# Turned products in the 64-wide attention heads: values stand in TensorE, the divided maps stream

## The reference, cut to what matters

```
p   = softmax(scores)            # rows: 128 queries, columns: up to 256 keys
out = p @ v                      # v: keys x 64
y   = out @ w_proj_a             # or w_out
```

## Time and profile before

| what | value |
|---|---|
| median of 3 runs | 1392.94 us (1392.09 to 1394.0) |
| profiled execution | 1392.42 us, span 1390.6 us |
| mean granted clock | 0.998 |
| PE busy | 99% of the span |
| DVE busy | 68% of the span |
| ACT busy | 51% of the span |

### The profile page before, as it was taken

How to read it: one execution, slowest core, us unless ns; L and a number is a source line. 1 busy time by engine, 2 the same in 40 slices (tenths; PEclk the granted TensorE clock), 3 DMA queues, 4 the chain that set the end, 5 groups by cost and what they waited for, 6 DMA issues and landing times.

```text
span 1390.6 us, 19203 instructions
## 1 busy us (share of the span) xinstructions
PE 1374.7 (99%) x7399; PEld 1170.1 (84%) x7399; DVE 943.3 (68%) x1161; ACT 712.6 (51%) x920; POOL 129.2 (9%) x141
## 2 busy tenths in 40 slices
PE   8999999999999999999999999999999999999999
PEld 7988888888888888888888888888888877788887
DVE  6895667666677666766567666766667778766665
ACT  5556436444455444576654444544445666554442
POOL 4100002000030000032020000200000321300000
PEclk9999999999999999999999999999999999999999
DMA  8644457655555556543255555466555532455562
GB/s 281 176 153 152 152 182 264 220 184 200 189 174 190 181 183 198 188 156 122 92 181 188 198 187 183 165 200 198 192 184 179 170 133 91 150 198 197 181 194 78
DMA packets 164859, 246.34 MB, mean 177 GB/s; under 512 B 4952, under 2 KB 121860, under 8 KB 164672
## 3 DMA queue, kind: packets, MB, share of 16 engines
q1 hardware_dynamic: 162256, 240.14, 51.5%
q0 software_dynamic: 1776, 4.74, 1.2%
q10 hardware_dynamic: 768, 0.66, 0.2%
HBM read 244.45 MB, written 1.07 MB: 177 GB/s over the span
## 4 chain that ended last, share of the span: by engine, by line
PE 91%; DVE 4%; ACT 2%; issue 1%; POOL 1%; DMA 0%; SPq 0%; ACTq 0%; POOLq 0%
PE ps L1542 27%; PE ps L1509 15%; PE ps L1547 14%; PE ps L1511 14%; PE ps L1510 14%; PE ps L1777 2%; PE ps L1748 1%; DVE wlo L901 1%; PE ps L1535 1%; ACT whi L552 1%; DVE xx L946 1%; ACT pr L617 1%; PE ps L2025 0%; DMA raw<-in_w_in 0%; ACT xx L589 0%
## 5 line engine op out<-in xcount | busy, mean ns | idle before, releaser
L1542 PE MATMUL ps<-xx,whi 128*128 128x512 f32 x1760 | 422.7, 391 | 1.6 <-DVE wlo L901 1.6
L1542 PEld LDWEIGHTS ps<-xx,whi 128*128 128x128 f32 x1760 | 325.4, 188 | 67.1 <-DVE wlo L901 2.6
L906 DVE TENSOR_TENSOR wlo<-raw,whi 128x2048 fp32r<-128x2048 f32 x120 | 275.1, 2293 | 94.2 <-ACT whi L560 94.2
L560 ACT ACTIVATE whi<-raw 128x2048 fp32r<-128x2048 f32 x120 | 229.6, 1913 | 122.4 <-PE ps L1511 122.4
L552 ACT ACTIVATE whi<-raw 128x2048 fp32r<-128x2048 f32 (+1 forms) x135 | 204.7, 1530 | 86.2 <-PE ps L1511 82.5
L1547 PEld LDWEIGHTS ps<-xx,wlo 128*128 128x128 f32 x1760 | 227.6, 191 | 9.9
L1547 PE MATMUL ps<-xx,wlo 128*128 128x256 f32 x1760 | 230.6, 283 | 0.0
L1509 PE MATMUL ps<-whi,hhi 128*128 128x512 f32 x504 | 198.6, 394 | 0.0
L1510 PE MATMUL ps<-wlo,hhi 128*128 128x512 f32 x504 | 196.7, 390 | 0.0
L1511 PE MATMUL ps<-whi,hlo 128*128 128x512 f32 x504 | 196.3, 390 | 0.0
L901 DVE TENSOR_TENSOR wlo<-raw,whi 128x2048 fp32r<-128x2048 f32 x75 | 171.4, 2287 | 24.8 <-ACT whi L552 24.7
(11 more groups left out here) (259 smaller groups left out, 1394.2 us busy)
## 6 DMA issues: line engine op xcount, KB each, us to landing
raw<-in_ffn_w_gate SPq DMA_DIRECT2D x44, 1024.0 KB, 5.2
raw<-in_ffn_w_up SPq DMA_DIRECT2D x44, 1024.0 KB, 5.1
raw<-in_ffn_w_down SPq DMA_DIRECT2D x44, 1024.0 KB, 4.8
raw<-in_w_in SPq DMA_DIRECT2D x40, 1024.0 KB, 5.1
raw<-in_w_gate_up SPq DMA_DIRECT2D x22, 1024.0 KB, 5.0
raw<-in_w_out SPq DMA_DIRECT2D x12, 1024.0 KB, 4.8
raw<-in_w_down SPq DMA_DIRECT2D x11, 1024.0 KB, 4.8
raw<-in_w_mem_kv SPq DMA_DIRECT2D x4, 1024.0 KB, 5.1
```

The source lines that it names most:

```text
L560: act.activation(whi[:, c % 3, :], raw[:, c % 3, :], ACT.Copy).then_inc(hi_done, 1)
L906: dve.tensor_tensor(wlo[:, c % 3, :], raw[:, c % 3, :], whi[:, c % 3, :], ALU.subtract)\
L1542: return pe.matmul(ps[:, bank + n, :], whi[:, slot, 256 * k + P * n:256 * k + P * n + P], both, start=start, stop=False)
```

## The change

- The list of A items runs over head pairs first and row tiles second, so that the first four items fill one bank.
- Items of kinds A and R, and X in layer 0 (24 items, `DIRECT`), are divided before they are turned: DVE's new `normalise(i)` makes the reciprocal of the two sums and multiplies the map in place. `item_turn` waits for it (`pn_ready`) and no longer for the exponential.
- In `item_pv` these items have v (128 keys x 64) standing and `pT` (128 queries) streaming. The heads e = 0 and 1 write the partitions 0 to 63 and 64 to 127 of one bank. The product comes out turned.
- The turns of `xn` in the first model (parts 0 and 1) and all four in layer 0 go, with the divisions in L1256 and L1440 for these items. ACT and DVE split straight from the product's bank (bank 7; bank 1 in layer 0). In the first model this is done in the iterations k = 5 and 9, where the divisions stood.
- In layer 0 the slots of turns and products move: `T_AT` is S + 3 for the first eight items, `V_AT` is S + 4 apart from items 8 to 11. Layer 1 stays as it was.

```diff
-ITEMS = [("A", rt, a, -1) for rt in range(RT) for a in range(AH // 2)]
+ITEMS = [("A", rt, a, -1) for a in range(AH // 2) for rt in range(RT)]
+DIRECT = [k in "AR" or (k == "X" and layer == 0) for k, _, _, layer in ITEMS]
+NORMED = np.cumsum(DIRECT).tolist()
-T_AT, V_AT = tuple(h + 2 for h in S_AT), tuple(h + 3 for h in S_AT)
+T_AT = (tuple(h + (3 if i < 8 else 2) for i, h in enumerate(S_AT)), tuple(h + 2 for h in S_AT))
+V_AT = (tuple(h + (3 if 8 <= i < 12 else 4) for i, h in enumerate(S_AT)), tuple(h + 3 for h in S_AT))
-Y_TURNS = ({40: 0, 43: 1, 53: 2, 57: 3}, {40: 0, 43: 1, 54: 2, 57: 3})
+Y_TURNS = {40: 0, 43: 1, 54: 2, 57: 3}
+Y_OUT = {V_AT[0][4 * g + 3] + 1: g for g in range(4)}
...
 # ScalarE, first model, after exps(k)
+                    if k in (5, 9):
+                        b = (k - 5) // 4
+                        act.wait_ge(pv_ready, 4 * b + 4)
+                        act.activation(hhi[:, b, :], ps[:, 7, :], ACT.Copy).then_inc(xhi_done, 2)
...
 # ScalarE, layer 0, at the head of a slot
+                    if L == 0 and h in Y_OUT:
+                        g = Y_OUT[h]
+                        act.wait_ge(pv_ready, i0 + 4 * g + 4)
+                        act.activation(y_hi_at[g], halves(ps[:, 1, :]), ACT.Copy).then_inc(y_hi, 1)
...
 # VectorE
+            def normalise(i):
+                kind, r, a, L = ITEMS[i]
+                nk = SEQ if kind == "X" else P * (r + 1)
+                total = sums[:, 2 * i:2 * i + 2]
+                v = halves(pr[:, i % 2, :])[:, :, 0:nk]
+                dve.wait_ge(p_ready, SOFT[i])
+                link(dve.reciprocal(total, total))
+                dve.tensor_tensor(v, v, total.unsqueeze(2).to_broadcast([P, 2, nk]), ALU.mult).then_inc(pn_ready, 1)
...
                 elif 7 <= u < 19:
+                    if 0 <= u - 8 < 8:
+                        normalise(u - 8)
                     scores(u - 7)
...
                     if k in (5, 9):
-                        link(dve.reciprocal(rec[:, 0:8], sums[:, 2 * i:2 * i + 8]))
-                        dve.wait_ge(pv_ready, i + 4)
-                        dve.tensor_tensor(xn[:, r, 0:512]..., ps[:, 7, :]..., rec[:, 0:8]..., ALU.mult)
+                        b = (k - 5) // 4
+                        dve.wait_ge(xhi_done, KC * T_Y0 + 2 * b + 2)
+                        dve.tensor_tensor(hlo[:, b, :], ps[:, 7, :], hhi[:, b, :], ALU.subtract).then_inc(xlo_done, 2)
...
                     if h in S_AT:
                         scores(i0 + S_AT.index(h))
+                    if L == 0 and h - 1 in S_AT:
+                        normalise(i0 + S_AT.index(h - 1))
...
 # TensorE, item_turn
+                elif DIRECT[i]:
+                    pe.wait_ge(pn_ready, NORMED[i])
                 else:
                     pe.wait_ge(p_ready, SOFT[i])
...
 # TensorE, item_pv
+                if DIRECT[i]:
+                    bank, col = 7 if L < 0 else 1, 256 * (a % 2) + P * r
+                    for b in range(nb):
+                        for e in range(2):
...
+                            c = P * (e * nb + b)
+                            ins = pe.matmul(ps[HD * e:HD * e + HD, bank, col:col + P], v, pT[:, i % 2, c:c + P],
+                                            start=(b == 0), stop=(b == nb - 1))
+                    ins.then_inc(pv_ready, 1)
+                    return
...
-                if u == 19:
-                    pe.wait_ge(sc_read, 12)
-                    pe.wait_ge(o_evac, 2)
-                    turn_part(T_Y0, 0, xn)
-                    turn_part(T_Y0, 1, xn)
...
-                    if h in Y_TURNS[L]:
-                        turn_product(Y_TURNS[L][h])
+                    if L == 1 and h in Y_TURNS:
+                        turn_product(Y_TURNS[h])
```

More of the change, by code:

```diff
@@ L585, in turned_gain @@
                     if c % 4 < 2:
-                        act.wait_ge(tr_ps, 4 * T + 2 * half + c % 2 + 1)
+                        act.wait_ge(tr_ps, turns_of(T) + 2 * half + c % 2 + 1)
                     else:
@@ L1283, in _ @@
                         lo(u + 3)
-                    if k == 12:
-                        for b in range(2):
-                            dve.wait_ge(xhi_done, KC * T_Y0 + 2 * b + 2)
-                            dve.tensor_tensor(hlo[:, b, :], ps[:, TURN_BANKS[T_Y0][b], :], hhi[:, b, :], ALU.subtract)\
-                                .then_inc(xlo_done, 2)
                     if 2 <= k < 6:
@@ L1410, in y_rest @@
                     dve.wait_ge(y_hi, 4 * L + g + 1)
-                    dve.scalar_tensor_tensor(out=y_lo_at[g], in0=halves(ps[:, Y_BANKS[g], :]),
+                    dve.scalar_tensor_tensor(out=y_lo_at[g], in0=halves(ps[:, Y_BANKS[g] if L else 1, :]),
                                              scalar=colg[:, 6:7] if L == 1 and g != 1 else 1.0, in1=y_hi_at[g],
@@ L1491, in _ @@
                         combine(i0 + S_AT.index(h))
-                    if h in V_AT and V_AT.index(h) % 4 == 3:
-                        group_out(V_AT.index(h) // 4)
+                    if L == 1 and h in V_AT[1] and V_AT[1].index(h) % 4 == 3:
+                        group_out(V_AT[1].index(h) // 4)
                 boundary(T_F2 + 3 * L, N_F2 + 3 * L, R_WO1 + 3 * L, WO[1 + L] + 3, None, FFU[2 + 2 * L])
@@ L1736, in item_turn @@
                     pe.wait_ge(pT_evac, i)
-                if L >= 0 and i - IT0[L] == 8:
+                if L == 1 and i - IT0[L] == 8:
                     pe.wait_ge(y_lo, 4 * L + 2)
@@ L1763, in item_pv @@
                     if g > 0 and (i - IT0[L]) % 4 == 0:
-                        pe.wait_ge(o_copied, 4 * L + g)
+                        if L == 0:
+                            pe.wait_ge(y_lo, g)
+                        else:
+                            pe.wait_ge(o_copied, g)
+                if DIRECT[i]:
+                    bank, col = 7 if L < 0 else 1, 256 * (a % 2) + P * r
+                    for b in range(nb):
+                        for e in range(2):
+                            h = 2 * a + e
+                            if kind == "X":
+                                v = kv[:, b, MW + HD * h:MW + HD * h + HD]
+                            elif L >= 0:
+                                v = z2[:, b, Z_V[g] + HD * h:Z_V[g] + HD * h + HD]
+                            else:
+                                v = z1[:, b, 2, HD * h:HD * h + HD]
+                            c = P * (e * nb + b)
[3 more added lines that the diff above has]
+                    return
                 for e in range(1 if kind == "D" else 2):
@@ L1774, in item_pv @@
                         else:
-                            v = z1[:, b, 2 if kind == "A" else 3, size * h:size * h + size]
+                            v = z1[:, b, 3, size * h:size * h + size]
                         c = P * (e * nb + b)
@@ L1927, in _ @@
                 pe.wait_ge(lo_done, u + 1)
+                if m == 0:
+                    pe.wait_ge(sc_read, 12)
                 if m == 1:
@@ L2017, in turn_heads @@
                         pe.wait_ge(heads_lo, 8 * L + k)
-                    if (g, which) == (3, "k"):
+                    if L == 1 and (g, which) == (3, "k"):
                         pe.wait_ge(y_lo, 4 * L + 1)
@@ L2053, in _ @@
                         item_scores(i0 + S_AT.index(h))
-                    if h in V_AT:
-                        item_pv(i0 + V_AT.index(h))
-                    if h in T_AT:
-                        item_turn(i0 + T_AT.index(h))
+                    if h in V_AT[L]:
+                        item_pv(i0 + V_AT[L].index(h))
+                    if h in T_AT[L]:
+                        item_turn(i0 + T_AT[L].index(h))
                     if h in HEAD_TURNS:
                         turn_heads(h)
-                    if h in Y_TURNS[L]:
-                        turn_product(Y_TURNS[L][h])
+                    if L == 1 and h in Y_TURNS:
+                        turn_product(Y_TURNS[h])
                 last_one(WO[1 + L] + 3, (4, 6), left(3), (y_lo, 4 * L + 4), T_F2 + 3 * L, R_WO1 + 3 * L)
```

50 lines of the change are left out of this document (22 added, 28 removed).

## The result

The changed kernel takes 1397.92 us (median of 6 runs, 1396.93 to 1399.73), the kernel before 1392.58 us in the same measurement (6 runs). The ratio is 1.0042, 95% interval 1.0032 to 1.0053: the medians lie 5.3 us apart, and the interval reaches from 4.5 to 7.4. I predicted 1398.5. Medians in this document are of executions in the usual state; two of the whole-array kernel in experiment 7 (1506 and 1941 us, mean granted clock 0.85 and 0.65) are left out.

A forecast was written before the change was run, and what follows sets the result against it. TensorE, busy 99% of the span, was taken as the bound. Products -0.8, turns -2.5, waits +7.7 and clock +1.7 gave +6.1 us on 1392.42: 1398.5 us, eight-in-ten range 1394 to 1407.5.

The forecast's parts named there:

- waits of items 0 to 5: First model: PE waits before turns for DVE's divisions, 2.8, 0, 0.8, 0.3, 0.5 and 3.3 us, +7.7 in all.
- turns: PE: eight transposes in the first model and sixteen in layer 0 go, -2.5 us.
- products: PE, 24 changed items: heads side by side, paying 0.2 or 0.3 us for the split array, -0.8 us.
- clock: PE's granted clock falls once behind the new long waits, +1.7 us (none 0, both +3.4).
- the circle over ACT and DVE: First model, items 1 to 4: scores, ACT's high part, DVE's low part, convolutions and division, then the turn; waits 0 to 0.8 us.
- The rival in which the normalising isn't late: First model: no waits on the division, only -0.8 and -2.5 us left, 1389.1 us; chance 0.11.
- the 0.31 of the scores: PE's scores, heads in two halves of the rows: going into the split array and out costs 0.31 us.
- One head after the other: Rival for the products on PE: pairs of records cost double, +8.4 us, 1406.9 us; chance 0.14.
- Bare pairs: Rival for the products on PE: the column split costs nothing, -6.8 instead of -0.8 us, 1392.5 us; chance 0.10.

The follow-up runs named there:

- experiment 7: The fifth version with both heads' values (128 columns) in the whole array, every sum started anew, half of each product thrown away: 1390.36 us (ten executions).
- experiment 8: The changed kernel with twelve transposes that nothing reads ahead of the turns of items 0 and 5: 1394.49 us, ratio 1.0016.
- experiment 4: The change in layer 0 alone, the first model as in the kernel before: 1388.43 us, ratio 0.9968.
- the fifth version: The changed kernel with the first model's divisions and bank 7 subtractions behind DVE's low part, and ScalarE's sine an iteration later: 1388.14 us, ratio 0.997.
- experiment 9: The changed kernel with only DVE's subtraction from bank 7 (k = 5 and 9) moved behind the low part: 1394.29 us, ratio 1.0013.
- experiment 3: The changed kernel with only item 0's division moved behind the low part: 1398.15 us, ratio 1.0039.
- experiment 1: The changed kernel with all the first model's divisions moved behind the low part of the same iteration, ahead of the convolutions: 1390.17 us, ratio 0.9977.
- experiment 11: The fifth version with the first model's products placed right behind the scores, ahead of the turns: 1386.09 us, ratio 0.9955.
- experiment 6: The fifth version with both heads' products in the same half of the array's columns, every sum started anew: 1395.58 us.
- experiment 2: The changed kernel with the first model's divisions and the subtraction from bank 7 both moved behind the low part: 1389.76 us, ratio 0.9975.

## Why the prediction was right

The sum, step by step. The measured values of work on PE come from distances inside one trace: item 0's turn to the end of the first model, and the stretch of layer 0.

| step | predicted | measured | from |
|---|---|---|---|
| waits of items 0 to 5 | +7.7 | +7.2 | waits of PE after |
| a wait of before that goes | not counted | -0.3 | item 1 waited 0.28 for its exponentials |
| turns | -2.5 | (-2.5) | not priced apart again |
| products | -0.8 | -2.5 | -5.0 in all, less the turns |
| clock | +1.7 | +3.4 | windows after; experiment 8 |
| sum | +6.1 | +5.3 | medians: +5.3 |

The traces close too. From the moment when PE is ready for item 0's turn to the first turn of layer 0 it is 534.51 us before (71.48 to 605.99) and 543.73 after (72.10 to 615.83), 9.2 more. Layer 0 is 4.0 less. That is +5.2, with the start of the kernel and layer 1 left out. That the median agrees to 0.1 is chance, since its interval is 2.9 us wide.

**The -5.0.** Layer 0 saves 4.03 (experiment 4). In the first model the fifth version takes 533.57 us with 0.32 of waiting, before 534.51 with 0.28: 0.98 saved. Together 5.0; less 2.5 for the turns, which were not priced apart again.

**The waits** were right item by item, within 0.2 us but for item 5, where 3.3 was predicted and 2.86 came. The causes were right too: item 0 waits for DVE's block of constants, items 2 to 5 for the circle over ACT and DVE, and item 5 also for ScalarE's copy (experiment 9). That they are one queue and not five separate waits is what experiment 3 adds: moving the first division alone doesn't pay, moving all of them does (experiment 1). What stands at the end of the queue can be taken out alone: item 5's wait got 1.8 us shorter and no other one longer (experiment 9). The rival in which the normalising isn't late predicted 1389.1; the kernel that makes it true comes to 1388.14.

**The products** were mis-sized: -0.8 in the sum, -2.5 measured. The heads run side by side with a cost for going in and out, as taken; the size of that cost is the term that was off. In the first model I took 0.3 and find 0.26, and had +0.3 us in all where 0.98 less 0.82 for the eight turns leaves -0.2. In layer 0 I took 0.2 for twelve items and 0.3 for four, 3.6 us together. It is 0.14 on the average of the sixteen, 2.3 together, and that 1.3 makes up the difference between the 1.1 us that I expected there and the 2.4 that came. It must, since the 0.14 is worked out from the 2.4. The 0.2 had no row behind it: I had the 0.31 of the scores and no case of two neighbours in a split array. The count was off as well: in the trace eleven of the sixteen products follow scores directly and five don't. An independent check comes from experiment 11, where standing next to the scores took 0.155 off the 0.26: 5 x 0.26 + 11 x 0.105 = 2.5, near the 2.3 found.

**The clock** went wrong the other way: two falls, not one, and 1.7 us each in this trace. I had the size right and the number by a guess between none and two. In the sum the two errors of 1.7 us cancel. By its own steps the forecast was right in its mechanism and lucky in its second digit: with the error of the clock alone it would have been 0.9 us from the measured time, with that of the products alone 2.5.

**The rivals.** One head after the other: experiment 6 makes it true, and costs 7.4 us by medians, and its 8.4 by the trace, 0.22 a pair. Bare pairs: experiments 6 and 7 find the cost of going in and out. The Trainium skill (TensorEngine Tiling (Array Packing), Theoretical Speedup) gives up to 2x for a dimension of 64; the pairs do run side by side, but a large item took 0.59 us instead of 0.82, not half. The Trainium skill says on the same page (Key Properties) that a change of mode drains the engine; the 0.26 us agree with a cost of that kind, and the 0.10 to 0.14 of layer 0, mostly beside scores, also a split, is less and not none. What in it is draining no run here shows.

**The profiled span** grew by 7.2 us and not 5.3: the execution reached item 0's turn 0.6 us later, and 1.4 us more were lost in the unchanged layer 1, where the same stretch takes 687.51 us before and 688.91 after. There PE waits 1.4 us at the same place in all 13 traces. In eight of them, before included, the clock falls at its end or up to 1.2 us behind it, and PE then waits for the exponentials of the next item for 0.3 us at most. In the other five the clock stays and PE waits 1.7 us there. Only in the profiled execution after does a fall follow that second wait as well, so it alone paid twice. The turns behind the 1.38 us before (0.69 us for two of them, at half the clock), then the same after (0.44), with the second wait:

```profile
1132.83 0.69 PE L1748 MATMUL ps<-cst,work 128*128 128x128 f32 x2 [1.38 <-DVE work L1055]
```

```profile
1138.63 0.44 PE L1771 MATMUL ps<-cst,work 128*128 128x128 f32 x2 [1.38 <-DVE work L1080]
...
1143.98 0.39 PE L1530 MATMUL ps<-heads_t 64*128 64x256 f32 x2 [1.69 <-ACT pr L627]
```

This is why the sum is closed against medians and against stretches of the traces, and not against the profiled span.

## What to carry to other kernels

When a step is put between two engines that hand over in a tight circle, ask first where in the in-order queue it stands, then what it costs: here 0.6 to 0.9 us of DVE work behind two convolutions cost PE 7.2 us of waits, and in front of them nothing that could be put down to it (the 1.8 us left at item 1 were ScalarE's). Removing the first wait of such a queue only moves it to the next item; move the step for all of them. The two long waits of TensorE here, 2.64 and 2.86 us, were paid twice, the second time in clock; try to break a wait that can't be removed with work that nobody needs; and put matmuls that use a split array next to each other.

## What the runs showed of the hardware

- Two products of 64 columns that stand in the two halves of the array's columns, each streaming the same 128 rows and 128 columns, overlap fully: 0.22 us for two products that take 0.44 in one half. They do so in either order, also when two of one head come before two of the other.
- Products of 64 columns in one half are no cheaper than products of 128 columns: 0.11 us a record in both, and with the way in and out 1.02 us against 0.81 for eight records.
- Idle stretches of 2.63, 2.64 and 2.86 us were each followed by the lower of the two clock levels (1.2 GHz of 2.4), 1.7 us of work lost each time. The stretch of 3.56 us in experiment 3 cost about twice that. Waits of 2.81 and 2.90 us with 1.5 us of dummy transposes at their head were not followed by it.
- Shorter ones went either way from execution to execution: 1.77 us was followed by a fall (experiment 1) and 1.78 at the same place was not (experiment 2); the 1.38 us in layer 1, with 0.95 two us ahead of them, were in eight of 13 traces. One trace with or without a fall behind a wait of this size proves nothing about the version.
- A sine between exponentials costs ScalarE two table loads of 1.28 us each.
